# Rotary embedding: halves turned by row transfers instead of a matmul, sine product on GpSimd

## The chip, the cores and the metric

The kernel runs on one core of a Trainium2 chip. A core has five engines that work side by side: TensorE (PE: matmuls), VectorE (DVE), ScalarE (ACT), GpSimd (POOL) and SyncE (SP, which here only starts transfers). The metric is device microseconds from start to end of one execution: the median of three runs.

## The reference

A transformer over 512 tokens of width 1024: a layer that mixes an indexed sparse attention with a three-branch attention (compressed, selected and window keys), a layer of differential attention, each with a squared-ReLU MLP, and a second model part with neighbourhood attention and a gated linear recurrence. The change touches only the rotary embedding, which the first two layers apply to queries and keys, heads of 64:

```python
def apply_rope(x, cos, sin):
    x1, x2 = jnp.split(x, 2, axis=-1)
    ...
    return jnp.concatenate([x1 * c - x2 * s, x2 * c + x1 * s], axis=-1)
```

## The kernel before

All data on the chip is feature-major here: a **unit** is 128 features (two heads) by 512 tokens, one feature a partition. A head's halves x1 and x2 lie in partitions 0 to 31 and 32 to 63 (64 to 95 and 96 to 127 for the second head). There are 31 units, each with the same steps:

1. TensorE projects it: 24 matmuls of 128x512 (8 pieces of the depth by 3 products of high and low parts) into a PSUM bank (`fm` or `products`, L463).
2. ScalarE copies the bank, scaled, into a buffer `P` in SBUF (L1138, L1315, L1711, L2021).
3. TensorE multiplies the copy by `rotm`, a 128x128 matrix of 0, 1 and -1, which exchanges the halves and sets the sign (L1114, L1308, L1689, L2010).
4. GpSimd multiplies the copy by the cosine table into `TT[2n]` (L1157, L1336, L1717, L2039).
5. VectorE multiplies the rotated unit, from PSUM, by the sine table into `TT[2n+1]` (L1172, L1324, L1723, L2053), and adds the two (L1176, L1327, L1726, L2057).

Every engine works through a list of its own, in order; an instruction waits on semaphores that others raise (`pe.wait_ge(*v_rope.at(name))` waits until VectorE has done `name`). The lists are written out by hand: generators that yield at steps, run after one another or interleaved.

The units by place:

- `pe_rope` with `r_index` (ki, qi0, qi1, ka), the first matmuls of the program; then the token projections (`pe_tokens`), the index scores, kc (`pe_kc`, followed on GpSimd by eight transfers of its shifted copies), `r_keys` (ks, kw) and `r_query` (qb0, qb1). VectorE meanwhile does the top-k rounds (L1290, L1292) and, before that, splits the tokens' weights.
- `ER`: qb2, qb3, then qa0 to qa3, run in quarters between the 52 steps of the even attention (`pe_er`, steps in `ER_AT`); VectorE adds at the step where the rotation was.
- `DR`: the 16 units dk0, dq0, ... dk7, dq7 of the differential attention. Each is two half-steps. Seven half-steps run first, the others one before each attention step (`pe_diff`, four steps a head). A step n of TensorE is: half a projection, the output product of step n-3, the transposes of step n-2, the scores of step n (from which VectorE takes the maximum, L2095, ScalarE the exponentials, L2108, VectorE the probabilities, L2116 to L2120).

Weights come by transfer into staging, and ScalarE and VectorE split each piece into a high and a low part (L394 and L398) before TensorE takes it. The banks for the projections of `DR` are 0, 1, 2, then always 6; bank 7 takes the rotation.

Of the kernel before, what the change touches and what calls it, by code (L numbers as in the profile page):

```python
# [12 lines left out]
ALU = mybir.AluOpType  # L13
# [3 lines left out]
T = 512  # L17
# [22 lines left out]
def shape_constants():  # L40

    c = {}
# [3 lines left out]
    c["c_sin"] = np.tile(np.sin(ang), (4, 1)).astype(np.float32)  # L46
    rot = np.zeros((128, 128), np.float32)
    for b in (0, 64):
        for d in range(32):
            rot[b + 32 + d, b + d] = -1.0  # L50
            rot[b + d, b + 32 + d] = 1.0
    c["c_rot"] = rot
# [63 lines left out]
def build(nc, ins, out):  # L116
    ctx = ExitStack()
    with ctx:
# [46 lines left out]
        rotm = sb("k_c_rot", [128, 128])  # L165
# [43 lines left out]
        piece_in = [signal(f"piece_in{i}", 16) for i in range(3)]  # L209
        masks_in, lev_in, w2_in = signal("masks_in", 16), signal("lev_in", 16), signal("w2_in", 16)  # L210
# [6 lines left out]
        p_mm, p_turn, p_rot = signal("p_mm"), signal("p_turn"), signal("p_rot")  # L217
# [6 lines left out]
        g_pow, g_cos, g_misc, g_hg = [signal(n) for n in ("g_pow", "g_cos", "g_misc", "g_hg")]  # L224
# [848 lines left out]
        class Rope:  # L1073


            def __init__(self, src, units, p0=0, after=None):
                self.src, self.units, self.p0, self.after = src, units, p0, after
# [23 lines left out]

        def pe_rope(pe, r, hook=None):
            w = None
            for n in range(len(r.units) + 2):
                if n >= 2:
                    m = n - 2
                    pe.wait_ge(*a_rope.at(r.units[m][0]))
                    if m >= 2:
                        pe.wait_ge(*v_rope.at(r.units[m - 2][0]))
                    elif r.after:  # L1110
                        pe.wait_ge(*v_rope.at(r.after))
                    else:
                        pe.wait_ge(*rope_in.at("rot"))
                    pe.matmul(bank[3 + m % 2], rotm, r.buf(m), start=True, stop=True).then_inc(*p_rot.next(r.units[m][0]))  # L1114
                if r.src and n == 0:
                    pe_first_two(pe, r)
                elif n < len(r.units) and (n > 1 or not r.src):
                    name, key, part, _, _ = r.units[n]
                    if part == 0:
                        w = take(pe, key)  # L1120
                    if n >= 3:
                        pe.wait_ge(*a_rope.at(r.units[n - 3][0]))
                    t = fm(pe, bank[n % 3], w, part * 128)
                    t.then_inc(*p_mm.next(("rope", name), *([("free", key)] if part else [])))
                    if hook:
                        hook(pe, n)
                yield

        def act_rope(act, r, hook=None):
            for n in range(len(r.units) + 1):  # L1130
                if n >= 1:
# [3 lines left out]
                    if m >= 5:  # L1135
                        act.wait_ge(*p_rot.at(r.units[m - 5][0]))
                        act.wait_ge(*g_cos.at(r.units[m - 5][0]))
# [9 lines left out]
        def pool_rope(pool, r):  # L1147
            for n in range(len(r.units)):
# [6 lines left out]
                else:  # L1155
                    pool.wait_ge(*rope_in.at("rot"))
                pool.tensor_tensor(TT[2 * n % 4][:, 0:T], r.buf(n), cosT, ALU.mult).then_inc(*g_cos.next(name))  # L1157
                yield

        def dve_rope(dve, r, hook=None):  # L1160
            for n in range(len(r.units) + 2):
                if n >= 2:
                    m = n - 2
                    name, _, _, dest, _ = r.units[m]
                    dve.wait_ge(*p_rot.at(name))
                    if m >= 2:
                        dve.wait_ge(*v_rope.at(r.units[m - 2][0]))
                    elif r.after:
                        dve.wait_ge(*v_rope.at(r.after))
                    else:  # L1170
                        dve.wait_ge(*rope_in.at("rot"))
# [2347 lines left out]
```

## Time and profile before

| | before |
|---|---|
| median of 3 runs | 2167.26 us (2166.97 to 2167.42) |
| span of the profiled execution | 2165.6 us |
| busy: TensorE / VectorE / ScalarE / GpSimd | 2108.2 / 1355.1 / 920.4 / 220.9 us |
| granted TensorE clock | nine tenths or more in all 40 slices |

The profile is one execution; its span runs from its first to its last instruction, and that is the profiled execution's own time as the page gives it. The median is 1.7 us above it. A page row names line, engine, operation, output and inputs, and the idle time before an instruction with what ended it. Busy time of TensorE is that of overlapping matmuls, so shorter pitches are read from the chain. Issues of transfers are not counted as busy.

### The profile page before, as it was taken

How to read it: one execution, taken by the hardware profiler on the slowest of the kernel's cores; microseconds unless marked ns; L12 is line 12 of the kernel's file. 1: busy time of each engine (PE TensorE's matmuls, PEld its weight loads, DVE VectorE, ACT ScalarE, POOL GpSimd, SP SyncE). 2: the span in 40 equal slices, each digit the busy share in tenths (PEclk: the TensorE clock that was granted, in tenths of full speed). 3: DMA queues.
4: the chain of work that ended last, by engine and by line, in shares of the span. 5: the costliest groups of instructions: out<-in, count | busy, mean ns of one | idle time of the engine just before them, and what ended most of it. 6: DMA issues, size and time to landing. Idle time of an engine off the chain costs nothing.

```text
span 2165.6 us, 27204 instructions
## 1 busy us (share of the span) xinstructions
PE 2108.2 (97%) x10819; PEld 1670.2 (77%) x10819; DVE 1355.1 (63%) x2004; ACT 920.4 (42%) x1494; POOL 220.9 (10%) x212
## 2 busy tenths in 40 slices
PE   8999999999999999899999999999999999999998
PEld 6765668888888767688888888666878768888887
DVE  4888646867834367757687554355645435768753
ACT  3235545454443244445445442244423224544542
POOL 2210000000000011100000003020335320000000
PEclk9999999999999999999999999999999999999999
DMA  7420113233232321123333324131111313233231
GB/s 186 120 59 21 21 40 103 83 107 117 80 115 82 98 59 40 39 88 106 108 97 100 107 86 115 58 93 40 59 59 39 98 59 107 100 115 98 97 101 75
DMA packets 163511, 182.64 MB, mean 84 GB/s; under 512 B 19701, under 2 KB 123562, under 8 KB 163386
## 3 DMA queue, kind: packets, MB, share of 16 engines
q1 hardware_dynamic: 160736, 174.00, 25.6%
q0 software_dynamic: 2320, 6.80, 1.2%
q8 instruction: 86, 1.41, 0.3%
q14 instruction: 39, 0.32, 0.0%
q10 hardware_dynamic: 330, 0.12, 0.0%
HBM read 177.75 MB, written 2.17 MB: 83 GB/s over the span
## 4 chain that ended last, share of the span: by engine, by line
PE 86%; DVE 9%; ACT 2%; issue 2%; DMA 0%; ACTq 0%; POOLq 0%; POOL 0%; DVEq 0%
PE banks L463 72%; PE banks L2900 3%; DVE wl L398 1%; ACT wh L394 1%; PE banks L3019 1%; PE banks L1608 1%; DVE big L1292 1%; PE banks L1644 1%; DVE sm L1555 1%; PE banks L1528 1%; DVE big L1598 1%; DVE m L1290 1%; PE banks L2086 1%; PE banks L2148 1%; PE banks L2669 1%
## 5 line engine op out<-in xcount | busy, mean ns | idle before, releaser
L463 PE MATMUL banks<-uTh,wh 128*128 128x512 f32 (+1 forms) x1424 | 552.8, 388 | 9.7 <-ACT p L2021 3.6
L463 PE MATMUL banks<-uTh,wl 128*128 128x512 f32 (+1 forms) x1424 | 538.6, 378 | 0.0
L463 PE MATMUL banks<-uTl,wh 128*128 128x512 f32 (+1 forms) x1424 | 538.2, 378 | 0.0
L463 PE MATMUL banks<-wh,hTr 128*128 128x512 f32 x1552 | 488.0, 392 | 0.3 <-DVE hTr L2208 0.3
L398 DVE TENSOR_TENSOR wl<-stg,wh 128x2048 fp32r<-128x2048 f32 x133 | 306.0, 2301 | 219.0 <-ACT wh L394 218.4
L463 PEld LDWEIGHTS banks<-wh,hTr 128*128 128x128 f32 x1552 | 291.8, 188 | 64.4 <-DVE wl L398 2.5
L394 ACT ACTIVATE wh<-stg 128x2048 fp32r<-128x2048 f32 x133 | 253.0, 1902 | 194.8 <-PE banks L463 175.7
L463 PEld LDWEIGHTS banks<-uTh,wh 128*128 128x128 f32 x1424 | 268.2, 188 | 63.7 <-issue 9.5
L463 PEld LDWEIGHTS banks<-uTh,wl 128*128 128x128 f32 x1424 | 268.2, 188 | 50.9
L463 PEld LDWEIGHTS banks<-uTl,wh 128*128 128x128 f32 x1424 | 268.6, 189 | 49.3 <-issue 2.4
L463 PE MATMUL banks<-wl,hTr 128*128 128x512 f32 x776 | 302.4, 390 | 0.0
L463 PEld LDWEIGHTS banks<-wl,hTr 128*128 128x128 f32 x776 | 146.0, 188 | 29.3
L870 ACT ACTIVATE p<-banks 128x512 f32<-128x512 f32 x96 | 57.4, 598 | 209.1 <-PE banks L463 209.1
L561 POOL TENSOR_TENSOR nrm<-nrm,half 128x1 f32<-128x1 f32 x28 | 16.6, 591 | 1169.5 <-DVE nrm L710 1145.9
L463 PE MATMUL banks<-wh,uTh 128*128 128x512 f32 (+1 forms) x256 | 100.4, 392 | 2.9 <-DVE big L2553 1.6
L888 DVE TENSOR_TENSOR hTr<-p,hTr 128x512 fp32r<-128x512 f32 (+1 forms) x132 | 78.9, 615 | 33.5 <-ACT hTr L883 33.3
L463 PE MATMUL banks<-wl,uTh 128*128 128x512 f32 (+1 forms) x256 | 98.2, 383 | 0.0
L463 PE MATMUL banks<-wh,uTl 128*128 128x512 f32 (+1 forms) x256 | 98.1, 383 | 0.0
L903 DVE TENSOR_TENSOR p<-p 128x256 f32<-128x256 f32 x36 | 15.2, 424 | 107.4 <-ACT p L872 107.4
L883 ACT ACTIVATE hTr<-p 128x512 fp32r<-128x512 f32 (+1 forms) x132 | 71.9, 564 | 19.7 <-DVE p L905 18.1
L974 DVE TENSOR_TENSOR h<-h,big 128x512 f32<-128x512 f32 x108 | 68.9, 688 | 0.3
L698 DVE TENSOR_TENSOR h<-h,banks 128x512 f32<-128x512 f32 x48 | 32.8, 685 | 51.1 <-PE banks L463 51.1
(383 smaller groups left out, 2793.4 us busy)
## 6 DMA issues: line engine op xcount, KB each, us to landing
stg<-mlp_w_up SPq DMA_DIRECT2D x32, 1024.0 KB, 5.3
stg<-mlp_w_down SPq DMA_DIRECT2D x26, 1024.0 KB, 5.1
stg<-w_in SPq DMA_DIRECT2D x20, 1024.0 KB, 5.2
stg<-w_up SPq DMA_DIRECT2D x16, 1024.0 KB, 5.3
stg<-w_down SPq DMA_DIRECT2D x13, 1024.0 KB, 5.1
stg<-odd_w_in SPq DMA_DIRECT2D x16, 512.0 KB, 4.8
big<-mlp_w_down SPq DMA_DIRECT2D x6, 1024.0 KB, 7.6
big<-even_cmp_w SPq DMA_DIRECT2D x4, 1024.0 KB, 5.6
```

Of the source, the lines that this page charges most:

```text
L394: act.activation(hi, source, ACT.Copy).then_inc(*a_hi.next(k))
L398: dve.tensor_tensor(lo, source, hi.bitcast(F32), ALU.subtract).then_inc(*v_lo.next(k))
L463: t = pe.matmul(outp, x, y, start=(start and k == 0 and m == 0), stop=(stop and k == n - 1 and m == 2))
L698: dve.tensor_tensor(hc, hc, bank[banks[c * 4 + i]], ALU.add).then_inc(*v_add.next((tag, c, i)))
L870: act.activation(r, up_bank(tag, j), ACT.Relu).then_inc(*a_up.next((tag, "relu", q, j)))
L883: act.activation(hi, v, ACT.Copy).then_inc(*a_up.next((tag, n, what)))
L888: dve.tensor_tensor(lo, v, hi.bitcast(F32), ALU.subtract).then_inc(*v_up.next((tag, n, what)))
L974: x = dve.tensor_tensor(hc, hc, v, ALU.add)
L1290: dve.max(m8[:, i - 1, :], s).then_inc(*v_top.next(("max", i, r)))
L1292: dve.match_replace(s, m8[:, i - 1, :], s, TAKEN).then_inc(*v_top.next(("taken", i, r)))
L1528: pe.matmul(b[:, g, :], qv[p, j, i * 128:(i + 1) * 128], kv[p, 0:w], start=True, stop=False)
L2900: t = pe.matmul(b, fill_w["y"][:, k, f * 128:(f + 1) * 128], (onT, ohT)[br][:, k, :], start=(k == 0), stop=(k == 3))
```

## The change

The rotation matmul and its matrix go. The exchange of halves is made by four transfers from the copy in SBUF to `TT[2n+1]`, 32 partitions of 2 KB each, issued by GpSimd right before the cosine product. GpSimd then multiplies them by a sine table that carries the sign, in loops of several units after the next unit's cosine product. VectorE only adds. In the index units, a split of token weights is done by VectorE ahead of ka's add; in `DR` the projections alternate between banks 7 and 6 from the fourth unit on, and the adds come one half-step later. Waits that named a rotation or a sine product now name the copy, the transfers or the add. The transfers raise one of two semaphores in turn.

```diff
-    c["c_sin"] = np.tile(np.sin(ang), (4, 1)).astype(np.float32)
-    rot = np.zeros((128, 128), np.float32)
...
+    c["c_sin"] = np.concatenate([-np.sin(ang), np.sin(ang)] * 2).astype(np.float32)
...
+        def pool_rotate(pool, n, name, src):
+
+            dest = TT[(2 * n + 1) % 4]
+            for b in range(4):
+                o = (b ^ 1) * 32
+                pool.dma_start(dest[b * 32:b * 32 + 32, 0:T], src[o:o + 32, :]).then_inc(
+                    *rot_in[n % 2].next(*([name] if b == 3 else [])))
...
         def pe_rope(pe, r, hook=None):
...
-                    pe.matmul(bank[3 + m % 2], rotm, r.buf(m), start=True, stop=True).then_inc(*p_rot.next(r.units[m][0]))
...
+                pool_rotate(pool, n, name, r.buf(n))
                 pool.tensor_tensor(TT[2 * n % 4][:, 0:T], r.buf(n), cosT, ALU.mult).then_inc(*g_cos.next(name))
-                yield
+                if n:
+                    pool_sin(pool, n - 1, r.units[n - 1][0])
+                if n == len(r.units) - 1:
+                    pool_sin(pool, n, name)
+                yield
+
+        def pool_sin(pool, n, name):
+
+            y = TT[(2 * n + 1) % 4][:, 0:T]
+            pool.wait_ge(*rot_in[n % 2].at(name))
+            pool.tensor_tensor(y, y, sinT, ALU.mult).then_inc(*g_sin.next(name))
+
+        def dve_turned_in(dve, n, name, dest):
+
+            x, y = TT[2 * n % 4][:, 0:T], TT[(2 * n + 1) % 4][:, 0:T]
+            dve.wait_ge(*g_cos.at(name))
+            dve.wait_ge(*g_sin.at(name))
+            dve.tensor_tensor(dest, x, y, ALU.add).then_inc(*v_rope.next(name))
...
         def dve_rope(dve, r, hook=None):
...
+                if r.src and n == N + 1:
+                    split("dve", r.units[2][1], 2)
+                if n >= 2:
+                    dve_turned_in(dve, n - 2, r.units[n - 2][0], r.units[n - 2][3])
                 yield
...
         def pool_kc(pool):
             pool.wait_ge(*a_rope.at("kc"))
             pool.wait_ge(*v_rope.at("ka"))
+            pool_rotate(pool, 0, "kc", r_kc.buf(0))
             pool.tensor_tensor(TT[0][:, 0:T], r_kc.buf(0), cosT, ALU.mult).then_inc(*g_cos.next("kc"))
+            pool_sin(pool, 0, "kc")
...
         def pool_er(pool, m):
...
+            pool_rotate(pool, m, name, er_buf(m))
             pool.tensor_tensor(TT[2 * m % 4][:, 0:T], er_buf(m), cosT, ALU.mult).then_inc(*g_cos.next(name))
+            pool_sin(pool, m, name)
 
         def dve_er(dve, m):
-            name, _, _, dest = ER[m]
-            dve.wait_ge(*p_rot.at(name))
...
+            dve_turned_in(dve, m, ER[m][0], ER[m][3])
...
         def dr_bank(m):
-            return bank[m] if m < 3 else bank[6]
+            return bank[m] if m < 3 else bank[7 - m % 2]
...
         def pe_dr(pe):
...
+                if m < 5:
+                    pe.wait_ge(*values_taken(m if m < 3 else 7 - m % 2))
+                else:
+                    pe.wait_ge(*a_rope.at(DR[m - 2][0]))
...
-                        pe.matmul(bank[7], rotm, dr_buf(m - 1), start=True, stop=True).then_inc(*p_rot.next(before))
...
+                    pool_rotate(pool, m - 1, name, dr_buf(m - 1))
                     pool.tensor_tensor(TT[2 * (m - 1) % 4][:, 0:T], dr_buf(m - 1), cosT, ALU.mult).then_inc(*g_cos.next(name))
+                    if m >= 2:
+                        pool_sin(pool, m - 2, DR[m - 2][0])
+                    if m == len(DR):
+                        pool_sin(pool, m - 1, name)
                 yield
                 yield
...
         def dve_dr(dve):
-            for m in range(len(DR) + 1):
+            for m in range(len(DR) + 2):
                 if m < len(DR) and DR[m][2] == 0:
                     split("dve", DR[m][1])
...
+                if m >= 2:
+                    dve_turned_in(dve, m - 2, DR[m - 2][0], DR[m - 2][3])
+                yield
                 yield
```

## Rows read from the trace of the kernel before

**Rows 1.** The page, parts 1 and 4: engines; the chain that ended last.
```profile
PE 2108.2 (97%) x10819; PEld 1670.2 (77%) x10819; DVE 1355.1 (63%) x2004; ACT 920.4 (42%) x1494; POOL 220.9 (10%) x212
...
PE 86%; DVE 9%; ACT 2%; issue 2%; DMA 0%; ACTq 0%; POOLq 0%; POOL 0%; DVEq 0%
```

**Rows 2.** Busy us (instructions) in a window: PE, PEld, DVE, ACT, POOL; clock, DMA.
```profile
736.00:877.00 141.00, 137.22 (x690) 99.17 (x688) 91.22 (x166) 59.97 (x145) 23.93 (x19) 1.00 0.21 60
```

**Rows 3.** The chain of waits in 0 to 300 us: start, length, what.
```profile
125.48 0.61 DVE t L1723
...
131.11 1.33 PE banks L1454 x32
```

**Rows 4.** Instructions that touch the rotation matrix, differential stage: durations min/median/max.
```profile
L2010 PE MATMUL banks<-p,k_c_rot x32: 591/592/697, 738.3 to 882.6; 128*128 128x512 f32 x32
```

**Rows 5.** The chain of waits in the differential stage.
```profile
798.20 0.86 PE banks L2010 x2
...
816.93 1.16 PE banks L463 x4
```

**Rows 6.** Instructions that touch the sine table, then the cosine table.
```profile
L2053 DVE TENSOR_TENSOR t<-banks,k_c_sin x16: 681/684/692, 739.4 to 889.2; 128x512 f32<-128x512 f32 x16
...
L2039 POOL TENSOR_TENSOR t<-p,k_c_cos x16: 1265/1286/1690, 736.5 to 884.4; 128x512 f32<-128x512 f32 x16
...
L3338 SPq DMA_DIRECT2D k_c_cos<-c_cos x1: 1601/1601/1601, 13.4 to 13.4; - x1
```

**Rows 7.** Timeline of GpSimd: first and last of kc's eight transfers.
```profile
78.20 0.57 POOL L1340 DMA_DIRECT2D big<-big  x1 [6.05 <-DVE big L1327]
...
81.82 0.55 POOL L1341 DMA_DIRECT2D big<-big  x1
```

**Rows 8.** Line 1341, four of those eight transfers: time from issue to landing.
```profile
DMA to landing us min/median/max: 2.7/3.1/4.0
```

**Rows 9.** Timeline of TensorE: first matmuls of two units, idle time before them.
```profile
795.20 0.47 PE L463 MATMUL banks<-uTh,wh 128*128 128x512 f32 x1 [0.52 <-ACT p L2021]
...
806.60 0.50 PE L463 MATMUL banks<-uTh,wh 128*128 128x512 f32 x1 [0.26 <-ACT p L2021]
```

**Rows 10.** The chain of waits in 24 to 64 us.
```profile
42.40 15.26 PE banks L463 x96
```

**Rows 11.** Timeline of VectorE: the split of the tokens' second piece.
```profile
44.44 1.60 DVE L398 TENSOR_TENSOR wl<-stg,wh 128x1392 fp32r<-128x1392 f32 x1
```

**Rows 12.** Timelines of GpSimd and VectorE around the add of kw.
```profile
88.01 1.26 POOL L1157 TENSOR_TENSOR t<-p,k_c_cos 128x512 f32<-128x512 f32 x1 [4.14 <-ACT p L1138]
...
90.53 2.56 POOL L1350 TENSOR_TENSOR q<-big,cols 128x512 f32<-128x512 f32 x2
...
90.53 3.12 DVE L1176 TENSOR_TENSOR big<-t 128x512 f32<-128x512 f32 x1
```

**Rows 13.** Timelines of VectorE and GpSimd at three of the even attention's units.
```profile
133.68 0.69 DVE L1723 TENSOR_TENSOR t<-banks,k_c_sin 128x512 f32<-128x512 f32 x1
...
235.35 0.69 DVE L1723 TENSOR_TENSOR t<-banks,k_c_sin 128x512 f32<-128x512 f32 x1
...
266.31 0.68 DVE L1723 TENSOR_TENSOR t<-banks,k_c_sin 128x512 f32<-128x512 f32 x1
...
130.41 1.33 POOL L1717 TENSOR_TENSOR t<-p,k_c_cos 128x512 f32<-128x512 f32 x1 [6.32 <-ACT p L1711]
...
229.55 1.27 POOL L1717 TENSOR_TENSOR t<-p,k_c_cos 128x512 f32<-128x512 f32 x1 [48.45 <-ACT p L1711]
263.64 1.28 POOL L1717 TENSOR_TENSOR t<-p,k_c_cos 128x512 f32<-128x512 f32 x1 [32.82 <-ACT p L1711]
```

**Rows 14.** Timeline of VectorE in the differential stage: a split, a late maximum.
```profile
799.26 2.29 DVE L398 TENSOR_TENSOR wl<-stg,wh 128x2048 fp32r<-128x2048 f32 x1
...
886.63 0.75 DVE L2095 TENSOR_REDUCE sm<-banks 128x1 f32<-128x256 f32 x2
```

**Rows 15.** Timeline of GpSimd in the differential stage: the row norm's power.
```profile
883.40 1.01 POOL L2184 TENSOR_TENSOR nrm<-nrm,half 128x4 f32<-128x4 f32 x1 [10.30 <-DVE nrm L2179]
```

More of the change, by code:

```diff
@@ L164, in build @@
         sinT = sb("k_c_sin", [128, T])
-        rotm = sb("k_c_rot", [128, 128])
         wi = sb("wi", [128, 16])
@@ L1100, in pe_first_two @@
             part(1, KT - 1).then_inc(*p_mm.next(("rope", r.units[1][0]), ("free", key)))
+        def pool_rotate(pool, n, name, src):
[4 more added lines that the diff above has]
+                    *rot_in[n % 2].next(*([name] if b == 3 else [])))
         def pe_rope(pe, r, hook=None):
             w = None
[L1104 to L1113, printed above, removed]
-                    pe.matmul(bank[3 + m % 2], rotm, r.buf(m), start=True, stop=True).then_inc(*p_rot.next(r.units[m][0]))
+            for n in range(len(r.units)):
                 if r.src and n == 0:
                     pe_first_two(pe, r)
-                elif n < len(r.units) and (n > 1 or not r.src):
+                elif n > 1 or not r.src:
                     name, key, part, _, _ = r.units[n]
@@ L1306, in pe_kc @@
             fm(pe, bank[5], w, 128, None).then_inc(*p_mm.next("vc", ("free", ("in", "kc"))))
-            pe.wait_ge(*a_rope.at("kc"))
-            pe.matmul(bank[3], rotm, r_kc.buf(0), start=True, stop=True).then_inc(*p_rot.next("kc"))
             yield
@@ L1322, in dve_kc @@
             take_more(5)
-            dve.wait_ge(*p_rot.at("kc"))
-            dve.tensor_tensor(TT[1][:, 0:T], bank[3], sinT, ALU.mult).then_inc(*v_rope.next(("kc", "sin")))
-            dve.wait_ge(*g_cos.at("kc"))
-            dve.wait_ge(*v_rope.now())
-            dve.tensor_tensor(kcT, TT[0][:, 0:T], TT[1][:, 0:T], ALU.add).then_inc(*v_rope.next("kc"))
+            dve_turned_in(dve, 0, "kc", kcT)
             dve.wait_ge(*g_misc.at("lev"))
@@ L1389, in pe_blocks @@
             pe.wait_ge(*(g_misc if hf else v_misc).at(("XP", c)))
-            if c and not hf:
-                pe.wait_ge(*a_misc.at(("cH", 0, 1)))
+            if not hf:
+                pe.wait_ge(*(a_misc.at(("cH", 0, 1)) if c else a_keep.at("vc")))
             xv = XP(c, hf).rearrange("p (s g n) -> p s g n", g=2, n=32)[:, :, :, hf:hf + 31]
@@ L1676, in er_buf @@
             return P[m % 2][:, 0:T]
-        def er_turned(m):
-            return bank[7] if m else bank[4]
         er_w = {}
@@ L2308, in pe_out1_half @@
                 elif i == 1:
-                    pe.wait_ge(*v_rope.at(("dq7", "sin")))
+                    pe.wait_ge(*a_rope.at("dk7"))
                 else:
@@ L3372, in pe_program @@
             pe_blocks(pe, 1, 1)
-            for x in range(3):
-                pe_er(pe, *divmod(2 + x, 3))
+            pe_er(pe, 1, 0)
+            pe_er(pe, 1, 1)
             run(pe_compressed(pe), pe_even(pe))
```

121 lines of the change are left out of this document (34 added, 87 removed).

## The prediction, made before the kernel after was run

> **What bounds the kernel now.** I read the page first, then busy time by stage, then the instructions that touch the rotation matrix and the two tables, then the chain of waits and the timelines around them. The page says that the time is TensorE's: it is busy 97% of the span, 86% of the chain that ended last, with VectorE 9% [rows 1]. So whatever leaves TensorE's queue counts nearly in full where TensorE sets the pace. The rotary embedding has 31 units: four index units, kc, two keys, two queries (24 to 120 us), six more in the even attention (120 to 268 us), sixteen in the differential stage (736 to 890 us). In that last stage TensorE is busy 137 of 141 us, VectorE 91 and GpSimd 24 [rows 2]: room on GpSimd, some on VectorE. Between 90 and 131 us the chain runs on VectorE (top-k rounds, a sine product at 125.48) and TensorE gets the compressed blocks at 131.11 [rows 3]. The units are thus of two kinds: on TensorE's path, or on VectorE's.
>
> **Change, part by part.** *Removed from TensorE:* a unit's rotation is two matmuls of 592 ns [rows 4] that overlap; in the chain they take 0.86 us together [rows 5]. All 31: 26.7 us.
> *Removed from VectorE:* a sine product, 0.68 us [rows 6]; I take 0.7 with its start. All 31: 21.7 us.
> *Added to GpSimd:* four row transfers, each to be issued on its own queue, and a second product. Eight such transfers start every 0.52 us (78.20 to 81.82) and hold the queue 0.55 each [rows 7], so four take 2.1. Those move 64 partitions, the new ones 32, so an issue could cost half if it goes by rows (0.27), or as much as the dearest issue among the tables' rows (1.60, the cosine table's load [rows 6]). I take 0.52, the same queue and kind, and keep both ends. Landing is 2.7 to 4.0 us from issue, median 3.1 [rows 8]. A product costs 1.29 us on GpSimd [rows 6], about 1.25 where two follow each other. So a unit costs GpSimd 2.1 + 1.25 + 1.25 = 4.6 us against 1.3 now; 31 add some 104 us on an engine with time to spare. What matters is when the result is there: a lone unit's last transfer is issued 1.6 us after the copy and lands at about 4.6, then the product: 5.8 us after ScalarE's copy. In the pipelined loops unit n's product stands behind unit n+1's four issues and cosine: 4.6 us after unit n+1's copy, its own transfers long landed. VectorE then waits at its add, and everything behind the add waits too.
> *Moved or freed:* the differential stage's projections alternate between banks 6 and 7, so TensorE no longer waits for ScalarE's copy before each unit (0.52 us before one, 0.26 before the next [rows 9]). The adds come half a unit later. The token split goes ahead of ka's add. Loading the rotation matrix goes away at 15 us, hidden now.
>
> **Index units and tokens.** TensorE works without a break through the four units to the tokens, which start at 42.40 and take 15.26 us [rows 10]. Without four rotations (3.5 us) the tokens start at 38.9 and want their second piece 7.6 us later, at 46.5. VectorE splits that piece at 44.44 now, in 1.60 us [rows 11]. After the change it stands behind qi1's add. On GpSimd, from the copy at 27.2: ki 2.1 + 1.25, qi0 the same, ki's sine, add at 36.0; then qi1's issues (they wait for that add), cosine and qi0's sine to 40.6, add 41.3; ka's issues and cosine to 44.7, qi1's sine to 46.0, add 46.7, split until 48.3. TensorE waits 1.8, and 1.7 of the 3.5 us are left.
> **kc to the gelu.** kc's rotation is on TensorE's path: 0.9 more, so kw's copy comes 2.6 earlier. It is at 88.0 now [rows 12]; GpSimd then needs issues, cosine and two sines, 5.9 us, and the add 0.7: 6.6 against the 5.6 until 93.65 now, 2.4 of which VectorE's add spends held by GpSimd: it takes 3.12 instead of 0.69, ending as GpSimd's 2.56 us of products do [rows 12]. Left: 1.6. VectorE, the bound from here, loses two sine products (qb0, qb1: 1.4) and about 0.5 of the same holding. It is then at qb2's add 3.5 us earlier, at 122.0, when GpSimd's result (after qb0's add at 116.2: 5.8 us) is just there; its sine product saves 0.7. Gain at 131.11: 4.0 us, rounded down from 4.2.
> **Even attention.** qb3: copy before GpSimd's 130.41, result at 136.2; VectorE is there at 133.68 [rows 13], waits 2.5 and saves 0.7; of the 1.8 I take 1.2 as lost, for TensorE has projections to do. qa0 to qa2: the tightest is qa2, 5.9 us between GpSimd's start at 229.55 and the add's turn at 235.35 [rows 13], against 5.8: no wait, 0.7 each gained, 2.1, as VectorE is on the chain there. qa3: copy at 263.6, add due at 266.31 [rows 13], result at 269.3: 3 us late less 0.7; the next steps have slack for most, and TensorE gains 0.86: minus 0.2. Sum +0.7.
>
> **Differential stage.** Before attention joins, TensorE alone sets the pace: three rotations and one bank wait of about 0.5 less, but the first scores wait about 1 us for dq0's later sine: 2.1. Then two units and four attention steps make a period of 21.73 us (795.20 to 816.93) [rows 5, 9]. TensorE loses 1.72 + 0.78 = 2.5: 19.2 if nothing else binds. VectorE: in the first step of a period it has two waits on others, the probabilities, a split of 2.29 us [rows 14], then the add. Counted from the end of the period's first scores: maximum, exponentials and probabilities to 3.1, split to 5.4; GpSimd has the row norm's power (1.01 us [rows 15]) to 1.9, issues to 4.0, and its cosine meets the split, as rows 12 show such meetings: I let it wait to 5.4, cosine to 6.7, sine to 7.9; VectorE's add to 8.6, scaling to 9.2, and only then the next maximum. ScalarE's exponential of it is needed for the second half of the scores after those: TensorE ends them at 10.9 instead of 10.2. The other two steps take 8.9. Period 19.8: a gain of 1.9, six times: 11.4. In the tail (877 us on) VectorE and latency rule. Its maximum at 886.63 comes after the probabilities and the scaling alone [rows 14]; now it has to wait for dk7's sine behind dq7's issues: power done at 882.9 (884.4 now; the total is 1.5 earlier without its sine and add), then 4.6 us, 887.5, add, scale: 2.2 late. One sine saved later 1.4 with its add, dq7's add 0.7 behind: minus 1.5. Sum of the stage 2.1 + 11.4 - 1.5 = 12.0.
>
> **Sum.** 4.0 + 0.7 + 12.0 = 16.7 us off the profiled span of 2165.6, which gives 2148.9; the runs' median is 1.7 above the span, and the launch around it isn't touched: 2150.6. What comes after each stage is TensorE's and moves along.
>
> GpSimd's page in the Trainium skill speaks against the change: "GPSIMD Engine Reference", sections 3 and 8, calls VectorE about twice as fast for two-input work, and says that the two share SBUF interfaces when VectorE has two SBUF inputs or uses its two-port modes. The first agrees with the rows (1.29 against 0.68), the second with the held add; by it the second rival below would come true. "DMA: Bandwidth & Descriptors", section "Anatomy of one DMA", has about 2.0 us fixed plus the bytes; by that a 64 KB transfer would land in some 2.2 us, an estimate, lone units would be 0.9 us earlier and the sum some 1.5 us larger.
>
> **Rivals.**
> 1. *Nothing waits for GpSimd.* For it: in the loops the transfers have a whole unit to land. Against: the places above where the add comes first. Then 3.5 + 0.9 + 3.9 (VectorE up to the gelu), 3.9 in the even attention, 2.6 + 0.5 + 15.0 + 1.4 in the differential stage: 32 us, 2135. Chance 0.12.
> 2. *Holding eats it.* Each further GpSimd product holds a two-input VectorE operation on the loop for its 1.29 us, as the add at 90.53 [rows 12]. Two products a period: 2.6 against the 1.9 left; six periods minus 4 instead of plus 11, other parts kept: 16.7 - 15.6 = 1.1 us, 2166; half of it, 2158. Against: only part of VectorE's operations have two SBUF inputs, and I have counted one such meeting. Chance 0.16 for 2158 to 2167.
> 3. *The issues are dearer (slower than before).* The place is the add in the first step of each period. Every us by which four issues exceed 2.1 delays the maximum behind it by that much: at 1.0 us an issue (4.0) the 1.9 is gone, at 1.6, which my upper bound allows (6.4, 4.3 more), a period is 2.4 longer than now, six times 14.4, and the 5.3 us gained elsewhere go into the same delay at the other adds: 2182. Against: all eight issues of the row take 0.55. Chance 0.08.
> 4. *Nothing changed,* TensorE's time being given back to other waits within 4.3 us. For it: a stage's waits overlap. Against: TensorE has 97% of the span. Time 2163 to 2171, chance 0.06.
>
> **Numbers.** My forecast, a gain of 9 to 27 us, has 0.58; it is 2150.6. The range, 2134 to 2164, takes in rival 1 and most of rival 2; it leaves out rivals 3 and 4 and what of rival 2 lies above 2164, together 0.19. Within 0.2% (4.3 us) is about what a measurement can't tell from no change: faster 0.82 (forecast, rival 1, three quarters of rival 2), same 0.10 (rival 4, the rest of rival 2), slower 0.08 (rival 3).
>
> **What would show it.** No 592 ns pairs and no sine product on VectorE; GpSimd busy some 261 us (its 221 and 31 products; issues are not counted); issues near 0.5 us; TensorE idle about 1.8 us before the tokens' second half, waiting for the split; VectorE idle before the adds of kw, qb3, qa3 and in the first step of each period, and a period of 19.8 us. Wrong if that period is under 19.3 (waits hidden) or above 21 (holding or issues), or if the top-k stretch shifts by under 2 us.

## The result, and the profile after

The changed kernel takes 2188.98 us (median of 4 runs, 2188.11 to 2191.70) against 2167.11 before (4 runs): 1.0094 times as long, 95% interval 1.0078 to 1.0109. It is 0.9% slower, where 0.8% faster was forecast. The profiled span went from 2165.6 to 2187.7 us: 22.1 more. The page's busy times and chain, the new issues and the landings (compare [rows 1, 7, 8]):

```profile
PE 2097.1 (96%) x10753; PEld 1669.4 (76%) x10757; DVE 1362.1 (62%) x1973; ACT 919.4 (42%) x1494; POOL 328.6 (15%) x367
PE 79%; DVE 9%; POOL 4%; issue 4%; ACT 3%; DMA 1%; ACTq 0%; POOLq 0%; DVEq 0%
L1101 POOL DMA_DIRECT2D t<-p x124 | 62.8, 513 | 245.4 <-ACT p L1699 129.1
t<-p POOLq DMA_DIRECT2D x124, 64.0 KB, 2.0
```

TensorE was relieved, and yet its share of the chain fell from 86% to 79%; GpSimd, which had 0%, has 4%, and "issue" 4% instead of 2%. An issue costs 0.51 us, as taken. The landing is 2.0 us in the median, better than the 3.1 taken. So the two unknown prices were right or on the safe side. The 62.8 us of issues also stand in GpSimd's busy time (328.6 us where 261 was forecast): the page does count them as busy on that engine. VectorE's busy time rose by 7.0 us although 31 products of 0.68 us are gone, so its other instructions took some 28 us longer in all. That is what is called holding here: an instruction of VectorE or GpSimd that lasts longer because the other engine works at the same time. The list of waits names the new one, VectorE's on GpSimd (us in all, times, longest):

```profile
DVE big L1167 <- POOL t L1160: 49.0, 13, 6.7
```

L1167 is the add, L1160 the sine product. 13 of the adds wait, 49.0 us in all.

**Where the 22.1 us lie.** ScalarE's copies of the units are milestones that every version has. The first copy of the differential stage starts at 735.78 before and at 747.71 after (11.9 late). Its first three gaps shrink by 2.7 us (16.32 against 19.02). From its fourth to its last copy it takes 133.08 instead of 126.60 (6.5 more). From the last copy to the end of the span it is 1290.6 instead of 1284.2 (6.4 more). 11.9 - 2.7 + 6.5 + 6.4 = 22.1.

**Tokens.** GpSimd's timeline, then VectorE's, then the first matmul of TensorE's second piece (compare [rows 11]):

```profile
41.95 2.01 POOL L1101 DMA_DIRECT2D t<-p  x4 [1.34 <-DVE big L1167]
43.97 1.30 POOL L1149 TENSOR_TENSOR t<-p,k_c_cos 128x512 f32<-128x512 f32 x1
45.22 2.49 POOL L1160 TENSOR_TENSOR t<-t,k_c_sin 128x512 f32<-128x512 f32 x2
```
```profile
46.60 1.68 DVE L1167 TENSOR_TENSOR big<-t 128x512 f32<-128x512 f32 x1 [5.20 <-POOL t L1160]
48.20 1.59 DVE L392 TENSOR_TENSOR wl<-stg,wh 128x1392 fp32r<-128x1392 f32 x1
```
```profile
49.85 0.66 PE L457 MATMUL banks<-wh,uTh 128*128 128x348 f32 x1 [4.11 <-DVE wl L392]
```

The add of qi1 was forecast for 46.0 to 46.7 and the split until 48.3. The add started at 46.60 but ran 1.68 us, until half a us after GpSimd's second sine product had ended at 47.7: the holding. The split ended at 49.8. TensorE's second piece had to wait 4.11 us for it, where 1.8 was forecast, and kc's copy came at 71.18 instead of 70.18, where the forecast had it 1.7 us earlier, at 68.5.

**Keys, queries, compressed blocks.** VectorE's adds of ks and kw came late and were held (compare [rows 12]), and then TensorE's piece for qb2, whose split stands behind them on VectorE:

```profile
92.97 4.62 DVE L1167 TENSOR_TENSOR big<-t 128x512 f32<-128x512 f32 x2 [6.00 <-POOL t L1160]
97.52 2.04 DVE L1346 TENSOR_TENSOR q<-big,cols 128x512 f32<-128x512 f32 x1
```
```profile
117.00 0.79 PE L457 MATMUL banks<-uTh,wh 128*128 128x512 f32 x1 [5.84 <-DVE wl L392]
117.59 0.63 PE L457 MATMUL banks<-uTl,wh 128*128 128x512 f32 x1
```

Kw's add ended at 97.6 instead of 93.65, and VectorE's top-k rounds began 5.0 us later than before (100.38 against 95.41), where the forecast had them earlier: one of the signs that the prediction had named for being wrong. The split of qb2's weights came at 114.66, and TensorE stood 5.84 us for it. Its next matmuls took 0.63 us each, at a granted clock of 0.50 between 117 and 121 us; the same matmuls in the trace of before, entered without that wait, took 0.39. Qb2's copy was at 124.65, 5.9 us late.

**Even attention.** Qb3 (compare [rows 13]): GpSimd, then VectorE, then the issues of 134 to 146 us with the median time to landing.

```profile
135.65 2.00 POOL L1101 DMA_DIRECT2D t<-p  x4 [3.69 <-ACT p L1699]
144.06 1.26 POOL L1160 TENSOR_TENSOR t<-t,k_c_sin 128x512 f32<-128x512 f32 x1 [5.12 <-DMA t<-p]
```
```profile
145.42 0.69 DVE L1167 TENSOR_TENSOR big<-t 128x512 f32<-128x512 f32 x1 [6.74 <-POOL t L1160]
```
```profile
stg<-even_w_out SPq DMA_DIRECT2D x2, 512.0 KB, 6.3
t<-p POOLq DMA_DIRECT2D x4, 64.0 KB, 6.6
```

The transfers started while SyncE's loads of the output weights kept the DMA engines busy, and took 6.6 us to land. (That the loads are the reason is shown by e5 below.) The attention's first maximum came at 146.14 instead of 135.09.

**Differential stage.** One period. GpSimd, VectorE, TensorE (compare [rows 9, 14, 15]), then TensorE's busy time and clock in four windows.

```profile
808.50 1.04 POOL L2154 TENSOR_TENSOR nrm<-nrm,half 128x4 f32<-128x4 f32 x1 [6.02 <-DVE nrm L2149]
809.51 2.11 POOL L1101 DMA_DIRECT2D t<-p  x4
811.63 3.32 POOL L2014 TENSOR_TENSOR t<-p,k_c_cos 128x512 f32<-128x512 f32 x1
814.91 1.25 POOL L1160 TENSOR_TENSOR t<-t,k_c_sin 128x512 f32<-128x512 f32 x1
...
831.03 1.04 POOL L2154 TENSOR_TENSOR nrm<-nrm,half 128x4 f32<-128x4 f32 x1 [6.02 <-DVE nrm L2149]
```
```profile
808.33 0.48 DVE L2065 TENSOR_REDUCE sm<-banks 128x1 f32<-128x128 f32 x2
...
811.28 2.54 DVE L392 TENSOR_TENSOR wl<-stg,wh 128x2048 fp32r<-128x2048 f32 x1 [0.86 <-ACT wh L388]
816.27 0.69 DVE L1167 TENSOR_TENSOR big<-t 128x512 f32<-128x512 f32 x1 [2.44 <-POOL t L1160]
816.88 0.68 DVE L2161 TENSOR_TENSOR big<-banks,nrm 128x512 f32<-128x512 f32 x1
...
822.84 2.41 DVE L2088 TENSOR_SCALAR big<-big,sm 128x384 f32<-128x384 f32 x1
```
```profile
817.62 1.12 PE L2168 MATMUL banks<-k_c_ident,big 128*128 128x128 f32 x4 [2.82 <-DVE big L2161]
```
```profile
806.00:812.00 6.00, 6.00 (x37) 4.77 (x36) 4.20 (x11) 4.02 (x9) 3.48 (x6) 1.00 0.16 36
812.00:817.50 5.50, 2.80 (x17) 2.29 (x15) 3.06 (x4) 0.00 (x0) 4.16 (x2) 0.99 0.51 139
817.50:823.00 5.50, 5.38 (x21) 3.62 (x22) 3.79 (x11) 3.88 (x12) 2.51 (x5) 0.70 0.42 101
823.00:829.00 6.00, 6.00 (x34) 4.31 (x35) 5.01 (x7) 1.94 (x7) 2.02 (x2) 1.00 0.05 11
```

The chain that the forecast wrote for the first step came true step by step: power, issues, a cosine product that meets the split (3.32 us instead of 1.3), the sine product, the add. What follows did not. The add is followed by the scaling of the row (L2161), and TensorE's turn of that row (L2168) stands ahead of its next scores. TensorE idles 2.82 us there; in the next 5.5 us its granted clock is 0.70, so part of it ran at the lower of its two levels (1.2 of 2.4 GHz). The period is 831.03 - 808.50 = 22.53 us, against 21.73 before and 19.8 forecast.

**Its end.** Dk7's add, with nothing behind it in the pipeline to hide it:

```profile
904.55 1.67 DVE L1167 TENSOR_TENSOR big<-t 128x512 f32<-128x512 f32 x1 [3.79 <-POOL t L1160]
```
```profile
906.88 1.11 PE L2168 MATMUL banks<-k_c_ident,big 128*128 128x128 f32 x4 [5.38 <-DVE big L2161]
```

The last add ends 16.7 us after the last copy (913.84 - 897.11); before it was 9.3 (890.67 - 881.40).

**TensorE's clock.** The mean granted clock of the profiled execution is 0.996 before and 0.985 after. Between the fourth and the last copy of the differential stage it is 1.00 before and 0.94 after, and there TensorE waits before its turn in each period (2.82, 2.10 and 1.67 us in three that follow each other). What the clock costs can be estimated from the kernel before, measured 21 times beside e1 to e4: its span is 2163.6 to 2164.9 us in the five executions with a mean clock of 0.996 and 2173.8 to 2174.5 us in the four with 0.991, so 0.005 goes with about 10 us. By this estimate the 0.011 is worth some 20 of the 22.1 us: the waits alone would about have used up the gain, and the loss beyond it came as a lower clock.

### The profile page after: what moved, and what is told of

Its sections match the earlier page's. It is cut to its first block, busy times and chain, and to the rows that moved or that the text cites. A ratio compares the mean times of both kernels' runs of the same rounds, so it can differ in the third digit from the quotient of the medians.

```text
span 2187.7 us, 27149 instructions
## 1 busy us (share of the span) xinstructions
PE 2097.1 (96%) x10753; PEld 1669.4 (76%) x10757; DVE 1362.1 (62%) x1973; ACT 919.4 (42%) x1494; POOL 328.6 (15%) x367
## 4 chain that ended last, share of the span: by engine, by line
PE 79%; DVE 9%; POOL 4%; issue 4%; ACT 3%; DMA 1%; ACTq 0%; POOLq 0%; DVEq 0%
PE banks L457 66%; PE banks L2870 3%; DVE wl L392 2%; POOL t L1101 2%; ACT wh L388 1%; PE banks L2989 1%; PE banks L1605 1%; POOL t L1160 1%; PE banks L1641 1%; PE banks L1524 1%; POOL t L2014 1%; DVE sm L1551 1%; DVE big L1167 1%; DVE big L1594 1%; PE banks L2610 1%
## 5 line engine op out<-in xcount | busy, mean ns | idle before, releaser
L392 DVE TENSOR_TENSOR wl<-stg,wh 128x2048 fp32r<-128x2048 f32 x133 | 313.4, 2356 | 223.8 <-ACT wh L388 223.4
L1101 POOL DMA_DIRECT2D t<-p x124 | 62.8, 513 | 245.4 <-ACT p L1699 129.1
```

Source lines behind the costliest of these rows:

```text
L392: dve.tensor_tensor(lo, source, hi.bitcast(F32), ALU.subtract).then_inc(*v_lo.next(k))
L1101: pool.dma_start(dest[b * 32:b * 32 + 32, 0:T], src[o:o + 32, :]).then_inc(*rot_in[n % 2].next(*([name] if b == 3 else [])))
```

## Experiments

Theory after the first profile: the sine product of unit n-1 stands on GpSimd behind the wait for unit n's copy, unit n's four issues and its cosine, and VectorE, in order, stands in front of the add. Rivals: the price of the issues, the landing, GpSimd's product with the holding, or a loss in one place only. In the table the ratio is the measure, since the kernel before took 2169.6 to 2172.0 us beside the experiments; the median stands there to be set beside each expectation. The other columns are from one profile each: kc's copy, the differential stage's first copy (start), fourth to last copy (stage), the granted clock between these two, last copy to the end of the span (rest). One profile is one execution: that of e4 was its slowest (2186.65 us, median 2180.36), so differences of a few us in start and rest are not read as effects.

| kernel | median, us | ratio to before | kc | start | stage | clock | rest |
|---|---|---|---|---|---|---|---|
| before | 2167.1 | 1 | 70.2 | 735.8 | 126.6 | 1.00 | 1284.2 |
| changed | 2189.0 | 1.0094 | 71.2 | 747.7 | 133.1 | 0.94 | 1290.6 |
| e1 sine product first | 2169.5 | 0.9999 (0.9983 to 1.0016) | 68.1 | 746.5 | 122.3 | 0.99 | 1281.3 |
| e2 sine product on VectorE | 2169.0 | 0.9988 (0.9975 to 1.0002) | 66.5 | 740.8 | 124.6 | 0.97 | 1284.3 |
| e3 new form in the differential stage only | 2177.7 | 1.0038 (1.0025 to 1.0051) | 70.3 | 736.1 | 133.4 | 0.94 | 1291.5 |
| e4 new form in the rest only | 2180.4 | 1.0049 (1.0032 to 1.0065) | 71.8 | 752.7 | 126.6 | 1.00 | 1286.6 |
| e5 output weights behind qb3 | 2184.2 | 1.0065 (1.0051 to 1.0079) | 72.6 | 743.1 | 133.2 | 0.94 | 1287.1 |
| e6 e3 with the sine product first | 2162.8 | 0.9970 (0.9957 to 0.9982) | 70.4 | 736.1 | 122.2 | 0.99 | 1285.6 |
| e7 sine product over 32 columns | 2157.6 | 0.9941 (0.9924 to 0.9957) | 66.4 | 739.4 | 118.0 | 1.00 | 1284.3 |
| e8 one transfer instead of four | 2162.6 | 0.9966 (0.9952 to 0.9979) | 66.1 | 738.5 | 116.2 | 1.00 | 1290.4 |
| e9 issues on ScalarE | 2181.0 | 1.0050 (1.0030 to 1.0070) | 67.5 | 752.4 | 122.0 | 1.00 | 1288.2 |
| e10 parts together | 2158.0 | 0.9947 (0.9933 to 0.9962) | 65.8 | 734.3 | 122.3 | 0.99 | 1281.6 |
| e11 sine product behind the wait | 2172.2 | 1.0012 (0.9998 to 1.0025) | 68.1 | 745.8 | 121.4 | 0.99 | 1284.8 |
| e12 add one step later | 2181.7 | 1.0049 (1.0031 to 1.0068) | 71.3 | 748.1 | 129.3 | 0.99 | 1287.3 |

**e1: order.** In the index, key and query loops and in the differential stage:

```diff
                     name = DR[m - 1][0]
+                    if m >= 2:
+                        pool_sin(pool, m - 2, DR[m - 2][0])
                     pool.wait_ge(*a_rope.at(name))
...
-                    if m >= 2:
-                        pool_sin(pool, m - 2, DR[m - 2][0])
                     if m == len(DR):
```

> GpSimd multiplies unit n-1 by the sine before it waits for unit n's copy, instead of after unit n's four issues and its cosine product; in the even query heads and for kc nothing changes, since these units stand alone. Theory (VectorE, in order, stands before an add whose sine product is behind the next unit's work): adds wait no more in the differential stage, its period falls from 22.53 us to 20 to 21 us, six periods give back 9 to 15 us, and kw and the queries give back 2 to 4: 2170 to 2178 us. Rival (the loss is holding at the shared SBUF access, as many bytes by GpSimd as before): the same work in another order, the time stays within 3 us of 2189. Rival (the transfers' landing or the issues themselves are what is waited for): the sine product now waits for the landing in the open, 2.0 us for each unit, and the time stays or rises.

The whole loss goes, by nothing but order: 21 us, more than the 11 to 19 expected. The two rivals of this run fall: as many issues, products and bytes as in the changed kernel, and as much holding (VectorE is busy 1361.9 us, against 1362.1). But the first copy of the differential stage is still 10.7 us later than before. That part of the loss is not cured by the order; it is outweighed by the shorter stage and rest.

**e2: the sine product on VectorE.**

```diff
         def dve_turned_in(dve, n, name, dest):
...
-            dve.wait_ge(*g_cos.at(name))
-            dve.wait_ge(*g_sin.at(name))
+            dve.wait_ge(*rot_in[n % 2].at(name))
+            dve.tensor_tensor(y, y, sinT, ALU.mult).then_inc(*v_rope.next((name, "sin")))
+            dve.wait_ge(*g_cos.at(name))
+            dve.wait_ge(*v_rope.now())
             dve.tensor_tensor(dest, x, y, ALU.add).then_inc(*v_rope.next(name))
```

> The transfers stay on GpSimd, and the product with the sine goes back to VectorE, which takes the landed rows from SBUF instead of a bank. Theory (late sine products on GpSimd): VectorE gets 31 products of 0.7 to 1.2 us back, but its adds wait for nothing, GpSimd's work for a unit falls by 1.25 us, and the splits of 2.3 us and the two-input products are held less: 2168 to 2178 us. Rival (VectorE's own time is what counts): 31 more products on it, 0.5 to 1 of each in the path: 2195 to 2205 us. Rival (issues and landing are the loss): within 3 us of 2189.

As the theory has it: 2169.0 us. The front, the part before the even attention, shows it best: kc's copy comes 3.7 us before that of before, which is what four rotations less on TensorE are worth (3.5) if the token split isn't late. The differential stage still starts 5.0 us late, and the place shows in ScalarE's copies: from qb3's to qa0's it takes 19.2 us before, 28.5 changed, 26.7 in e1 and 26.6 in e2. There qb3's transfers land, which e5 takes up.

**e3 and e4: one place or both.** e3 is the kernel before with the differential stage's functions of the changed one; e4 the reverse. For both the turning matrix has 1 where it had -1, since the sine table has the signs.

> The kernel before, with the new form in the differential stage alone (with the two banks in turn there). From the shifts of the trace the stage lost 10 us (12.1 us late at its first copy, 22.1 at the end): 2176 to 2179 us. Rival (a gain of this stage that is eaten by the granted clock after the earlier delays, or a loss that lies in one stage only): 2167 or under, or 2185 and over.

> The changed kernel, with the form of before in the differential stage alone. From the shifts: tokens 1.4, kc and its followers 3.5, the second half of the compressed blocks none, qb3 6, qa3 2.8, altogether 12 to 14 us: 2179 to 2181 us. Together with the run that has the new form in the differential stage alone it must add up to 2189; if these waits only move work that was hidden before the MLP, it is 2170 or under.

Both medians, 2177.7 and 2180.4 us, are as expected. 0.38% and 0.49% add up to 0.87% of the 0.94%: both places lose, about equally, and hardly through each other.

**e5: the landing.** SyncE waits for qb3's transfers before it loads the first piece of the output weights:

```diff
             kts, ncols, parts, _ = SPEC[key]
+            if key == ("out0", 0, 0):
+                sp.wait_ge(*rot_in[1].at("qb3"))
```

> The changed kernel, but SyncE starts the loads of the first piece of the output weights (2 MB) only when qb3's four transfers have landed. Theory (qb3's landing of 6.8 us stands behind these loads, and the even attention's first maxima stand behind qb3's add): the landing falls to about 2 us, qb3's add comes 4 us after its copy instead of 10, the first maximum at 141 instead of 146.1; the time falls by 4 to 5 us, to about 2184. Rival (the attention catches up, or the later piece holds the output product): 2187 to 2190.

GpSimd's timeline, then VectorE's:

```profile
137.54 2.01 POOL L1103 DMA_DIRECT2D t<-p  x4 [3.69 <-ACT p L1701]
...
141.95 1.29 POOL L1162 TENSOR_TENSOR t<-t,k_c_sin 128x512 f32<-128x512 f32 x1 [1.10 <-DMA t<-p]
```
```profile
143.34 0.69 DVE L1169 TENSOR_TENSOR big<-t 128x512 f32<-128x512 f32 x1 [2.77 <-POOL t L1162]
```

The wait for the landing falls from 5.12 to 1.10 us, and the stage starts 4.7 us earlier. From qb3's copy to qa0's it takes 20.6 us now, near the 19.2 of before, and so too in e10 (20.7), which has the same edit. The ratios differ by 0.29%, some 6 us, with intervals that just meet; the median, 2184.2, is the expected one. So the landing is a part of the loss, at one unit: 5 to 6 us.

**e6: e3 with the order of e1.**

> The kernel before; in the differential stage alone the new form, with the sine product of unit n-1 ahead of the wait for unit n's copy. In the changed kernel with this order everywhere, the stage's first copy came 10.8 us late and its end 0.8 us late, so the stage gained 10; alone it should give 2155 to 2159 us, faster than both kernels, with a period of 20.5 us. Rival (part of that gain was only catching up of work that was late from the front): 2162 to 2167, a period of 21 or more.

VectorE's timeline, then GpSimd's:

```profile
793.85 3.27 DVE L399 TENSOR_TENSOR wl<-stg,wh 128x2048 fp32r<-128x2048 f32 x1
797.04 1.77 DVE L1122 TENSOR_TENSOR big<-t 128x512 f32<-128x512 f32 x1
```
```profile
791.06 1.04 POOL L2192 TENSOR_TENSOR nrm<-nrm,half 128x4 f32<-128x4 f32 x1 [6.02 <-DVE nrm L2187]
792.09 1.27 POOL L1115 TENSOR_TENSOR t<-t,k_c_sin 128x512 f32<-128x512 f32 x1
793.31 2.06 POOL L1108 DMA_DIRECT2D t<-p  x4
795.38 2.87 POOL L2054 TENSOR_TENSOR t<-p,k_c_cos 128x512 f32<-128x512 f32 x1
798.22 1.71 POOL L1115 TENSOR_TENSOR t<-t,k_c_sin 128x512 f32<-128x512 f32 x1
...
811.63 1.04 POOL L2192 TENSOR_TENSOR nrm<-nrm,half 128x4 f32<-128x4 f32 x1 [6.01 <-DVE nrm L2187]
```

The add waits no more (but for 1.3 us, once), and the period is 811.63 - 791.06 = 20.57 us, as expected. It is faster than the kernel before, by 6.5 us (0.30%), less than the 10 or so expected; the median of 2162.8 us lies in the range of the rival, though the period is the theory's. The 10 us had been read from the last part of e1, whose "rest" was 4 us shorter. Held work remains: the split takes 3.27 us instead of 2.3, the add 1.77 instead of 0.69, where GpSimd multiplies.

**e7 and e8: GpSimd's time for a unit, cut at two different ends.** e7 makes the sine product over 32 columns of 512, so that most of the sine is left out; e8 moves all 128 rows in one transfer, so that the halves aren't exchanged:

```diff
-            pool.tensor_tensor(y, y, sinT, ALU.mult).then_inc(*g_sin.next(name))
+            pool.tensor_tensor(y[:, 0:32], y[:, 0:32], sinT[:, 0:32], ALU.mult).then_inc(*g_sin.next(name))
```
```diff
-            for b in range(4):
-                o = (b ^ 1) * 32
-                pool.dma_start(dest[b * 32:b * 32 + 32, 0:T], src[o:o + 32, :]).then_inc(
-                    *rot_in[n % 2].next(*([name] if b == 3 else [])))
+            pool.dma_start(dest[:, 0:T], src).then_inc(*rot_in[n % 2].next(name))
```

> The changed kernel; the product with the signed sine is made over 32 of 512 columns only (the output leaves out the rest of the sine), so that the waits and their order stay and the work of 1.25 us for each of 31 units falls to about 0.2. Theory (an order that puts each sine product behind the next unit's copy, issues and cosine): the adds come 1 us earlier but wait still; 2180 to 2184 us. Rival (the product itself and the holding between GpSimd and VectorE is the loss): 2168 to 2173 us, as with the sine on VectorE.

> The changed kernel with one transfer of 128 rows for each unit instead of four of 32 (the halves are not exchanged, which the output shows), so the same bytes with a quarter of the issues. Theory: GpSimd is busy with issues for 0.5 us instead of 2.0 for each unit, and what stands behind it, the cosine and the sine product of the unit before, comes 1.5 us earlier: 2178 to 2183 us. Rival (the issues are the loss): 2168 to 2172. Rival (the landing alone counts): 2187 to 2190.

Here the gains that the theory expected were far too small, and even the times of the rivals that blamed the product or the issues (2168 to 2173) were passed: the medians are 2157.6 and 2162.6 us. A product shorter by 1.0 us, 31 times, gave 1.53%, 33 us; 1.5 us less of issues gave 1.28%, 28 us. That is 1.1 us of the kernel for each us of product and 0.6 for each us of issues: no fixed exchange. Neither the issues nor the product is the loss by itself, for either cut does; GpSimd's length ahead of an add is, until VectorE's turn is reached (in e7, still in the stage, its add waits 1.46 us for GpSimd and the period is 20.3). Holding is a part of what e7 won and not of what e8 won: VectorE is busy 1344.5 us in e7, 17.6 less than in the changed kernel, and 1361.4 in e8. In the front e7 and e8 bring kc's copy to 66 us: with about one us less on GpSimd the token split is no longer late.

**e9: the issues moved off GpSimd.** ScalarE issues the four transfers right behind its copy, once the buffer is free:

```diff
                     act.activation(dr_buf(m - 1), dr_bank(m - 1), ACT.Copy, scale=scale).then_inc(*a_rope.next(name))
+                    act.wait_ge(*a_rope.now())
+                    if m >= 3:
+                        act.wait_ge(*v_rope.at(DR[m - 3][0]))
+                    act_rotate(act, m - 1, name, dr_buf(m - 1))
```

> The changed kernel, but the four transfers of each unit are issued by ScalarE right behind its copy, not by GpSimd; the sine product stays on GpSimd, in the same order, behind the next unit's cosine. The runs with one transfer (2163) and with the narrow product (2158) say that GpSimd's own length from the copy to the sine product decides, whatever part of it is cut. Theory now: GpSimd is rid of 2.0 us for each unit, the period falls to 20.1 to 20.4 us and the time to 2160 to 2166, if an issue on ScalarE costs under 0.2 us. Rival: an issue costs ScalarE what it costs GpSimd, 0.5 us, and ScalarE with 2 us more for each unit makes the exponentials late: 2180 to 2195 us. Rival (the run with one transfer won by its fewer and larger transfers, by the landing): 2180 or more too, with landings of 2 us or more that the sine products wait for.

```profile
808.16 2.44 ACTq L1101 DMA_DIRECT2D t<-p  x4
810.70 0.37 ACT L2090 ACTIVATE big<-banks,sm 128x128 f32<-128x128 f32 x1 [2.57 <-issue]
```

The rival came true, with a median of 2181.0 us: an issue costs ScalarE 0.6 us, more than GpSimd, and the exponential behind the four stands for 2.57. In the stage it is still the better place (122.0 us against 133.1), but its first copy comes at 752.4, 4.7 later than in the changed kernel, though qa3's copy comes at the same time (274.15). Between 268 and 313 and between 313 and 358 us TensorE's granted clock is 0.96 and 0.96, where that of the changed kernel is 1.00. This is not shown to come from the edit: e4, whose code up to there is that of the changed kernel, has 0.92 and 0.96 in the same stretches and its first copy at 752.7.

**e11 and e12: the wait or the work, GpSimd's order or VectorE's.** e11 puts the sine product between the wait for the copy and the issues. e12 leaves GpSimd as it is and takes VectorE's add one step later:

```diff
                     split("dve", DR[m][1])
+                yield
                 if m >= 2:
                     dve_turned_in(dve, m - 2, DR[m - 2][0], DR[m - 2][3])
-                yield
                 yield
```

> The changed kernel; GpSimd makes the sine product of unit n-1 behind its wait for unit n's copy, but ahead of unit n's four issues and cosine product. The runs so far took 20 us off with the product ahead of the wait, 26 us with 1.5 us less of issues, 31 us with 1.0 us less of product. Theory (each us that GpSimd spends between unit n's copy and the end of unit n-1's sine product is a us of the kernel, until VectorE's add is ready when its turn comes): this order takes 3.3 to 5.3 us out of that stretch and leaves the wait for the copy in, which then costs nothing: within 4 us of the run with the product ahead of the wait, 2166 to 2172. Rival (the wait for the next copy is what made the adds late): little of the gain comes, 2180 to 2188.

> The changed kernel; in the differential stage VectorE makes each unit's add one step of the stage later (behind the scaling of the rows and the next maxima), GpSimd's order stays. Theory (VectorE stands before an add that is not ready, and what is queued behind it, the scaling for TensorE's turn, comes late): the wait of 2.4 us in each period goes, the period falls from 22.5 to 20.5 to 21 us, six periods give 9 to 12 us: 2177 to 2181. Rival (GpSimd's whole length bounds the period, so the wait only moves): the period stays above 22, 2186 to 2190; or the scores then wait for the late add, with the same sum.

```profile
831.71 0.49 PE L2056 MATMUL banks<-big 64*128 64x128 f32 x4 [2.15 <-DVE big L1167]
```

Both medians, 2172.2 and 2181.7 us, lie at the upper edge of what the theory expected. e11 gives back 18 of e1's 21 us: the wait for the next copy was nearly innocent, the issues and the cosine ahead of the product were the cause. e12 gives back 10 us by the ratio (6.7 by the profiles) with GpSimd's work and order untouched, its periods 21.2 and 21.0 us (copies at 799.95, 821.10, 842.10). So what counts in the stage is what stands behind VectorE's waiting add, the scaling and TensorE's turn. It isn't free: the scores of the next head now wait 2.15 us for the late add (TensorE's timeline).

The clock column goes with these waits. In three successive periods TensorE stands before its turn for 1.7 to 2.8 us in the changed kernel and in e3 and e5, which have the same stage, and the clock is 0.94 in all three. It stands for 1.7 or less in e11, for 0.8 to 1.3 in e1 and e6 (0.99), and for 1.1 or less in e7, e8 and e9 (1.00); e2, with 0.8 to 2.2, has 0.97. So a stage that avoids the wait wins twice.

**e10: the best version.** Sine product on VectorE before the MLP, on GpSimd and first in the differential stage, the output weights behind qb3.

> The parts that each gained by themselves: transfers everywhere, the sine product on VectorE for all units before the MLP, on GpSimd ahead of the wait for the next copy in the differential stage, and the first loads of the output weights behind qb3's landing. Sum: with the sine on VectorE the first copy of the differential stage came at 740.8 (before 735.8, changed 747.7); the loads held back gave 4.7 us on the changed kernel, so 736.5 to 737; the stage in the new order takes 122.2 us for its fourth to last copy instead of 126.6, less 2 us for its first copies: the end 5 to 6 us ahead of before, 2160 to 2164 us. Rival (the loads held back and the sine on VectorE give back the same wait once): 2164 to 2168 us.

It beats both kernels, and the expectation (2160 to 2164 us) as well: 2158.0 us, 0.9947 of before, 11.5 us. The stage starts at 734.3, and stage and rest take what they took in e1.

## Why the prediction was wrong

- *Prices:* right. Issue 0.51 (taken 0.52), product 1.25, no sine product on VectorE. GpSimd's busy time came out at 328.6 us, not 261: I had taken issues as not counted, and they are on GpSimd. The landing (2.0 in the median) was below the value taken, but at qb3 it was 6.6, and I had not asked what else the DMA engines carry at that moment. e5 puts 5 to 6 us on it; the even attention, +0.7 in the forecast, lost.
- *Index units and tokens, 1.7 us of gain left:* the failed step is "ka's issues and cosine to 44.7, qi1's sine to 46.0, add 46.7, split until 48.3". Ka's issues started half a us behind the add that they wait for (ended 41.40, first issue 41.95), and qi1's add was held for 1 us by the next product, a meeting that I had priced elsewhere but not here. TensorE then stood 4.11 us instead of 1.8, and 1.7 won became 1.0 lost at kc's copy.
- *kc to the gelu, 4.0 of gain:* the step "6.6 against 5.6" for kw took over the tokens' gain and assumed the holding away. From the end of kw's copy (88.04) to the end of its add it took 9.55 us, not 6.6, for both adds were held (4.62 us for two), and kw's add ended 3.9 late. What is late next was missing: qb2's split on VectorE, and TensorE behind it, 5.84 us plus matmuls at the lower clock.
- *Differential stage, period 19.8:* "and only then the next maximum" is where it failed. The chain up to the end of the add, written as 8.6 us, was right (808.33, the first maximum, to 816.96: 8.6). But behind the add stands the scaling, and TensorE's turn of the row is queued ahead of the next scores. I let the delay reach TensorE through the exponential only, 0.7 us; it idled 2.82, and then had a granted clock of 0.70. Add to it VectorE's work on the fourth step's probabilities, which took 2.41 us instead of 0.48 beside GpSimd's products. e6 shows that the stage can have 20.6 with all of the change in it.
- *TensorE's clock, put at nothing:* the sum has no term for it, since the page of before shows nine tenths or more everywhere. By the estimate above it is the largest single term, some 20 us between the two kernels, and in the differential stage it comes and goes with the waits that I had made too small.
- *Tail, minus 1.5:* the same error; 6.4 us were lost by the profile from the last copy to the end, and the lower clock is a part of them. Adds one unit later have nothing to hide behind at the end.
- *Rivals:* the slower side was given to dearer issues, 0.08. The issues were not dearer; the same place, the add in the first step of each period, decided all the same, with the prices that I had. So the chance for the slower side rested on a cause that did not occur. The second rival, holding, came true in its amount, some 28 us or 0.9 for each further product, but it isn't what decided: e1 has as much of it and is 21 us faster.
- By the Trainium skill ("GPSIMD Engine Reference", section 8) the two engines share SBUF interfaces, and contend when VectorE has two SBUF inputs or uses a two-port mode; the trace agrees, in both directions here: GpSimd's cosine 3.32 us instead of 1.3 beside a split, VectorE's split 3.27 instead of 2.3 beside a product.

What stays open: why the work behind the last copy takes between 1281 and 1292 us in kernels whose code there is the same. A part is the last adds (16.7 us after the last copy in the changed kernel, 12.3 in e1), and a part is the clock: added up from the trace, TensorE is at the lower of its two levels for 29 us of that stretch in the changed kernel, 15 before and 15 in e1. What lowers it so far behind the stage was not traced. Nor is it shown what a kernel with the changed order and no fall of the clock would take: the 20 us are an estimate from executions of another kernel.

## What to carry to other kernels

When work moves to an idle engine, write down not its busy time but the time from its input to the instruction that waits for its output, and put the finished half of a software pipeline ahead of the next unit's wait, issues and product: that order alone was worth 21 us here (1.0094 to 0.9999). For each instruction that may wait on an in-order engine, follow what is queued behind it to TensorE. Where TensorE waits, ask what its clock does next, and give that a term of its own. A forecast that finds a result due at the same moment as its reader (qb2's sine product and the add, both at 122.0) has no margin and should be counted as a loss risk: here that add waited 2.12 us.

## What the runs showed of the hardware

- A transfer of 64 KB between SBUF rows lands in 2.0 us in the median and in 6.6 beside loads of 512 KB pieces; its issue takes 0.50 us on GpSimd with 32 rows, 0.55 with 64, 0.6 with 128, and 0.6 on ScalarE with 32.
- Holding goes both ways: GpSimd's two-input product 1.3 to 3.3 us, VectorE's split 2.3 to 5.2 (at 755.58, beside two products), its add 0.69 to 2.9, and its one-input scaling of the probabilities 0.48 to 2.4 over 384 columns and 0.35 to 3.1 over 128. These are the longest of the changed kernel.
- TensorE's idle 2.8 us was followed by a granted clock of 0.70 over 5.5 us; its idle 5.8 us by a clock of 0.50 over 4 us and matmuls of 0.63 us instead of 0.39.
